# Last stage of a hybrid mixer and expert layer: earlier gathers, residual sums on GpSimd, the last tile stored in halves

## The reference, cut to what matters

```python
out = out + gates[:, e:e + 1] * (he @ p['w_exp_down'][l, e]).astype(f32)   # for each expert e
...
y = _moe(h, l, p)
x = x + gt2 * _rmsnorm(y, p['g_post_ffn'][l])
return x, s_f, s_b
```

## Time and profile before

| | us |
|---|---|
| median of 3 runs | 1619.06 (1616.66 to 1621.87) |
| the profiled execution | 1618.71 |
| its span | 1616.9 |
| TensorE matmul busy | 1392.7 (86%) |
| VectorE busy | 744.0 (46%) |
| ScalarE busy | 238.9 (15%) |
| GpSimd busy | 76.6 (5%) |

### The profile page before, as it was taken

How to read it: one execution, slowest core, us unless ns; L and a number is a source line. 1 busy time by engine, 2 the same in 40 slices (tenths; PEclk the granted TensorE clock), 3 DMA queues, 4 the chain that set the end, 5 groups by cost and what they waited for, 6 DMA issues and landing times.

```text
span 1616.9 us, 13844 instructions
## 1 busy us (share of the span) xinstructions
PE 1392.7 (86%) x5196; PEld 644.3 (40%) x5196; DVE 744.0 (46%) x1245; ACT 238.9 (15%) x390; POOL 76.6 (5%) x127
## 2 busy tenths in 40 slices
PE   2679959999999899999999989589989887899780
PEld 0135524444555445555544434433333333333330
DVE  0135785885776887977873756600000000000005
ACT  0211220100011021111221001411101110111013
POOL 4000000000001000000000000000000000000001
PEclk9799979999999999999999999789989989999995
DMA  9996246675559643122326733999989999999985
GB/s 332 414 358 208 95 146 227 232 244 188 170 176 335 202 142 111 59 85 90 125 97 241 241 135 107 417 348 414 399 335 394 403 403 406 401 406 384 408 357 202
DMA packets 131199, 421.92 MB, mean 261 GB/s; under 512 B 8130, under 2 KB 73893, under 8 KB 113253
## 3 DMA queue, kind: packets, MB, share of 16 engines
q1 hardware_dynamic: 118100, 375.78, 61.4%
q0 software_dynamic: 6656, 32.61, 6.1%
q10 hardware_dynamic: 6384, 12.73, 2.2%
HBM read 409.53 MB, written 23.09 MB: 268 GB/s over the span
## 4 chain that ended last, share of the span: by engine, by line
PE 59%; DMA 21%; DVE 13%; issue 3%; ACT 3%; ACTq 1%; POOLq 0%; SPq 0%; DVEq 0%; POOL 0%
PE ps L497 17%; PE ps L494 14%; DMA s_mem<-in_w_exp_gate 12%; PE ps L823 11%; DMA s_mem<-in_w_ada 7%; PE ps L843 6%; DVE s_mem L1439 4%; DVE s_mem L1604 2%; PE ps L441 1%; PE ps L663 1%; DMA s_mem<-in_hy_freq 1%; DVE s_mem L1576 1%; PE ps L614 1%; PE ps L423 1%; PE ps L625 1%
## 5 line engine op out<-in xcount | busy, mean ns | idle before, releaser
L1439 DVE SCALAR_TENSOR_TENSOR s_mem<-s_mem,s_sT 128x512 f32<-128x512 f32 x480 | 339.4, 748 | 56.8 <-DMA s_mem<-in_w_ada 45.4
L494 PE MATMUL ps<-s_mem 128*128 128x384 f32 x1024 | 343.1, 492 | 1.1 <-DVE s_mem L1470 1.1
L497 PE MATMUL ps<-s_mem 128*128 128x512 f32 x768 | 339.8, 601 | 0.7 <-ACT s_mem L1256 0.7
L823 PE MATMUL ps<-s_mem 128*64 128x512 f32 x1152 | 261.6, 611 | 34.8 <-DMA s_mem<-in_w_exp_gate 34.2
L494 PEld LDWEIGHTS ps<-s_mem 128*128 128x128 f32 x1024 | 193.5, 192 | 142.5 <-issue 18.3
L497 PEld LDWEIGHTS ps<-s_mem 128*128 128x128 f32 x768 | 146.3, 193 | 184.8 <-issue 183.7
L823 PEld LDWEIGHTS ps<-s_mem 128*64 128x64 f32 x1152 | 88.2, 141 | 205.4 <-issue 204.5
L1868 DVE TENSOR_TENSOR s_mem<-s_mem,ps 64x512 f32<-64x512 f32 x18 | 12.2, 680 | 325.4 <-ACT s_mem L1330 325.4
L843 PE MATMUL ps<-s_mem 128*64 128x512 f32 x576 | 152.4, 690 | 9.3 <-DVE s_mem L1870 9.3
L843 PEld LDWEIGHTS ps<-s_mem 128*64 128x64 f32 x576 | 45.5, 157 | 103.0 <-issue 91.1
L1152 ACT ACTIVATE s_mem<-ps 128x512 f32<-128x512 f32 (+1 forms) x61 | 34.4, 581 | 338.3 <-PE ps L497 172.4
(11 more groups left out here) (258 smaller groups left out, 931.9 us busy)
## 6 DMA issues: line engine op xcount, KB each, us to landing
s_mem<-in_w_ada SPq DMA_DIRECT2D x128, 512.0 KB, 5.0
s_mem<-in_w_exp_up SPq DMA_DIRECT2D x32, 2048.0 KB, 33.0
s_mem<-in_w_exp_gate SPq DMA_DIRECT2D x32, 2048.0 KB, 25.8
s_mem<-in_w_exp_down SPq DMA_DIRECT2D x32, 2048.0 KB, 29.5
s_mem<-in_w_in SPq DMA_DIRECT2D x24, 2048.0 KB, 8.8
s_mem<-in_w_ada SPq DMA_DIRECT2D x16, 2048.0 KB, 12.6
s_mem<-in_w_out SPq DMA_DIRECT2D x8, 2048.0 KB, 8.1
y_slots<-s_mem ACTq DMA_DIRECT2D x36, 256.0 KB, 11.2
```

Of the source, the lines that this page charges most:

```text
L494: m = mm(ps[:, banks[m_], 0:TOK], v[:, k, m_ * P:(m_ + 1) * P], hT[:, kk, :], start=(kk == 0), stop=(kk == KT - 1))
L497: m = mm(ps[:, banks[m_], :], hT[:, kk, m_ * P:(m_ + 1) * P], v[:, k, :], start=(kk == 0), stop=(kk == KT - 1))
L823: m = mm(ps[half, 0, :], hgT[:, kh * 8 + k, :], weights(e, 2 * kh + which)[:, k, :], start=(kh + k == 0), stop=(kh * 8 + k == KT - 1), ski ...
L1439: v.op(ve.scalar_tensor_tensor(out=o, in0=w, scalar=scale, in1=o, op0=ALU.mult, op1=ALU.add), S("piece_used") if last else None)
```

## The change

It changes the last stage on four engines.

- GpSimd waits for load 94 in place of load 95, gathers the early rows of tiles 0 and 1, and behind the last block's rows the late rows of both, then tile 2. It takes over the weighing of tile 2 (`last_weighed`) and the residual sums of tiles 0 and 1 (`rows_added`).
- ScalarE weighs tiles 0 and 1 at once; behind the root of each it waits for VectorE's reciprocal (`root_ready`) and scales the tile by it (`z_scaled`).
- VectorE's order becomes combine 0, reciprocal 0, combine 1, reciprocal 1, combine 2, reciprocal 2, and the residual pass of tile 2 in two halves of 1024 columns. Its residual passes of tiles 0 and 1 are gone.
- SyncE stores tiles 0 and 1 behind GpSimd's sums, and tile 2 in two halves.

```diff
 # SyncE
-            for t in range(NT):
-                sp.wait_ge(S("out_ready"), t + 1)
+            for t in range(2):
+                sp.wait_ge(S("rows_added"), t + 1)
                 sp.dma_start(out_rows[t], yga[t][0]).then_inc(S("out_done"), 16)
-            sp.wait_ge(S("out_done"), 16 * NT)
+            for half in range(2):
+                c = slice(half * (D // 2), (half + 1) * (D // 2))
+                sp.wait_ge(S("out_ready"), half + 1)
+                sp.dma_start(out_rows[2][:, c], yga[2][0][:, c]).then_inc(S("out_done"), 16)
+            sp.wait_ge(S("out_done"), 16 * (NT + 1))
 # GpSimd
-            i = LOADS_A_EXPERT * NE - 1
+            i = LOADS_A_EXPERT * NE - 2
             pool.wait_ge(S(f"w{i % len(MOE_SLOTS)}"), 16 * (i // len(MOE_SLOTS) + 1))
-            gather_y(early_i, range(1))
-            for r in range(2):
-                pool.wait_ge(S(f"y_gathered0{r}"), 16)
+            gather_y(early_i, range(2))
+            for t in range(2):
+                for r in range(2):
+                    pool.wait_ge(S(f"y_gathered{t}{r}"), 16)
             pool.wait_ge(S("y_stored"), nblk * 32 + 1)
             pool.nop(nofuse=True)
-            gather_y(late_i, range(1))
-            gather_y(slot_i.rearrange("p r t -> p (r t)"), range(1, NT))
+            gather_y(late_i, range(2))
+            gather_y(slot_i.rearrange("p r t -> p (r t)"), range(2, NT))
+
+            pool.wait_ge(S("y_gathered20"), 16)
+            g.op(nc.gpsimd.tensor_scalar(yga[2][0], yga[2][0], wpair[:, 0, 2:3], None, ALU.mult), S("last_weighed"))
+            for t in range(2):
+                pool.wait_ge(S("z_scaled"), t + 1)
+                g.op(nc.gpsimd.tensor_tensor(yga[t][0], yga[t][1], x_sb[:, t, :], ALU.add), S("rows_added"))
 # ScalarE
             def weigh(t):
-                act.wait_ge(S(f"y_gathered{t}0"), 32 if t == 0 else 16)
+                act.wait_ge(S(f"y_gathered{t}0"), 32)
                 a.op(A(yga[t][0], yga[t][0], ACT.Copy, scale=wpair[:, 0, t:t + 1]), S("y_weighed"))
 
             weigh(0)
+            weigh(1)
             for t in range(NT):
-                if t + 1 < NT:
-                    weigh(t + 1)
                 act.wait_ge(S("y_added"), t + 1)
                 squares(yga[t][0], y_sb[:, 0, :], 32 + t)
                 roots(32 + t, 1, D)
+                if t < 2:
+                    act.wait_ge(S("root_ready"), t + 1)
+                    a.op(A(yga[t][1], yga[t][1], ACT.Copy, scale=stat[:, 32 + t:33 + t]), S("z_scaled"))
 # VectorE
-                dve.wait_ge(S("y_weighed"), t + 1)
+                if t < 2:
+                    dve.wait_ge(S("y_weighed"), t + 1)
+                else:
+                    dve.wait_ge(S("last_weighed"), 1)
                 y0, y1 = yga[t]
-                dve.wait_ge(S(f"y_gathered{t}1"), 32 if t == 0 else 16)
+                dve.wait_ge(S(f"y_gathered{t}1"), 32 if t < 2 else 16)
...
-            def add_residual(t):
+            for t in range(2):
+                combine(t)
                 inverse_roots(32 + t, 1)
-                v.op(ve.scalar_tensor_tensor(out=yga[t][0], in0=yga[t][1], scalar=stat[:, 32 + t:33 + t],
-                                             in1=x_sb[:, t, :], op0=ALU.mult, op1=ALU.add), S("out_ready"))
-
-            combine(0)
-            for t in range(1, NT):
-                combine(t)
-                add_residual(t - 1)
-            add_residual(NT - 1)
+                v.sync()
+                dve.sem_inc(S("root_ready"), 1)
+            combine(2)
+            inverse_roots(34, 1)
+            for half in range(2):
+                c = slice(half * (D // 2), (half + 1) * (D // 2))
+                v.op(ve.scalar_tensor_tensor(out=yga[2][0][:, c], in0=yga[2][1][:, c], scalar=stat[:, 34:35],
+                                             in1=x_sb[:, 2, c], op0=ALU.mult, op1=ALU.add), S("out_ready"))
```

## The result

The change makes the kernel slower, by a third of a per cent: 1623.69 us median of 13 runs against 1619.06 us median of 13 runs of the kernel before on the same chip, ratio 1.0035 (95% interval 1.002 to 1.005), 5.7 us. Forecast was 1620.0 and no measurable change.

A forecast was written before the change was run, and what follows sets the result against it. The 33.7 us tail was taken as set by the gathers' landing, VectorE's passes and 2 MB of final stores. Profiled 1618.71 us plus 1.3 gave 1620.0, range 1614.6 to 1623.0 us.

The forecast's parts named there:

- the exclusion: A VectorE instruction with two SBUF inputs and a GpSimd instruction reading SBUF exclude one another for the whole instruction.
- part 4: GpSimd's passes in the tail: weighing of tile 2 at 2.0 us, residual sums at 4.5 us each, taking turns with VectorE.
- the 1.3 forecast: End of the span: 2 MB of stores from 1611.4 take 6.8 us, ending at 1618.2, 1.3 us over 1616.9.
- Part 1: Waiting for the last load but one, tile 1 gathered early: gathers start about 1564.7, cost 0, unless the load disturbed.
- Rival D: Early gathers and last load disturb one another; 1620.3 us in all; no separate chance, counted with the forecast.
- part 3: ScalarE and VectorE on tiles 0 and 1: new 1.9 us stall before tile 1, whose passes run 1595.55 to 1600.25.
- Part 2: GpSimd's gathers behind 1583.16: tile 1 complete near 1591.0, no longer 1595.8; long 2.76 us issue read as exclusion.
- A: GpSimd's arithmetic and VectorE's two-input passes do not exclude each other in the tail: 1616.2 us, chance 0.28.
- B: GpSimd takes both sums back to back, VectorE's first pass of tile 2 waits until 1609.0: 1621.2 us, chance 0.15.
- C: GpSimd's sums are cheap, near 1.8 us each, so exclusion hardly bites: 1613.0 to 1614.0 us, chance 0.10.

The follow-up runs named there:

- the pairs: Changed kernel plus, behind its last store, GpSimd sums or multiplies each beside three VectorE passes; a sum lengthened three two-SBUF-input passes by 4.1 us (11.11).

## Why the prediction was wrong

It had the order of events, the exclusion and the price of a sum, and missed the size: the time lies 0.7 us above its range.

**The step that failed** is part 4's "For the weighing of tile 2 (one stream in, one out) I take 2.0 us, from 1.8 to 3.6". Measured: 5.44 us. I had priced streams, by the memset; a copy does cost 1.89, but the multiply costs more than the two-input sum. Behind the landing, the weighing was to be done after 16.75 us and was after 20.36 (1601.21): 3.6 us. Everything behind it moved on: tile 2's first pass ended after 27.0 us, not 23.7; sum 1 after 31.4, not 28.2. The range did not carry this term at all: its bounds were worked out from the sum's price, 3.6 to 5.4 us, with the weighing at 2.0 throughout. Even the bound "from 1.8 to 3.6" would have been short by 1.8 us.

**The second term** was not in the sum at all: I had the end 6.85 us behind sum 1, set by the stores. The stores did land 6.55 us behind it, but the end of GpSimd's list set the span, 8.08 us behind it: 1.2 us. 3.2 and 1.2 are the 4.4 us between the forecast tail (35.0) and the measured one (39.45); with the 1.3 forecast, the 5.7. The tails bear both out. With the weighing off GpSimd the tail shrinks by 4.8 us, and with a bare wait at the end of GpSimd's list it grows from 31.0 to 34.9.

**Part 1** held: the gathers alone are worth 2.6 to 2.8 us of tail. But they don't start 0.95 us behind the last load but one (landed 1561.5). The wait that ends last is now the rows of the last block but one:

```profile
1565.25 1.05 POOL L1075 DMA_INDIRECT s_mem<-y_slots,s_early_i  x1 [51.60 <-DMA y_slots<-s_mem]
```

They were there in time all the same, and no matmul waited. Rival D said that part 1 is "worth little more than part 3's stall costs". In the changed kernel it is so: the stall eats it, and tile 1's first pass starts 12.7 us behind the landing, as before (12.75; 10.2 with the gathers alone).

**Part 2 and the exclusion** held; the long gather issue came again (2.78 us), beside the two-input pass, as it was read. **Part 3** held to 0.3 us: stall 2.00, forecast 1.9. **Sum** 4.49, forecast 4.5.

**Rivals.** A (no exclusion) is refuted by the pairs. B did not happen: VectorE's waiting pass ran between the sums each time. Its 1621.2 to 1623.0 us were nearest to the measured time by luck. C is refuted by 4.49 us.

## What to carry to other kernels

Price an operation on GpSimd by that operation in a trace, not by its streams: here a multiply by a scalar costs 5.4 us for 128x2048, more than a sum (4.5) and 2.9 times a copy (1.9). The Trainium skill (GPSIMD Engine Reference, "Engine selection") has one-input operations on GpSimd at roughly line rate; the copy agrees (1.89 us, where ScalarE's weighing takes 2.00), the multiply does not. Moving sums to GpSimd was no relief for VectorE here, whose passes with two SBUF inputs and GpSimd's sums exclude each other; the nine passes on VectorE alone end sooner. Let GpSimd's list end early: in this kernel the execution ends 8 us behind it at the earliest. The best version found is the gathers alone, 2.6 to 2.8 us of tail and 0.11 and 0.12% of time below before, a gain that neither interval tells from none.

## What the runs showed of the hardware that I had not expected

The multiply's price and GpSimd's 8 us, above. And TensorE's clock: ahead of the tail, the same 32 matmuls behind the last gate load took 7.09 us in the kernels before and after, and 10.07 in the first trace with the weighing on ScalarE.

```profile
1560.86 10.07 PE L823 MATMUL ps<-s_mem 128*64 128x512 f32 x32 [3.13 <-DMA s_mem<-in_w_exp_gate]
...
1556.00:1560.00 4.00, 1.72 (x9) 0.29 (x4) 0.00 (x0) 0.00 (x0) 0.00 (x0) 1.00 1.03 437
1560.00:1564.00 4.00, 3.15 (x8) 1.11 (x10) 0.00 (x0) 0.00 (x0) 0.00 (x0) 0.51 1.00 423
1564.00:1568.00 4.00, 4.00 (x14) 1.28 (x12) 0.00 (x0) 0.00 (x0) 0.00 (x0) 0.64 0.98 409
```

The granted clock (third figure from the end, of full speed 2.4 GHz) fell to the lower level, 1.2 GHz, behind a wait of 3.13 us for the load; the kernel before waited 3.13 us at the same place and kept 1.00, and the second trace of the very same kernel waited 3.25 us, kept 1.00 and took 7.09. No kernel changed anything there. So two executions can differ by 3 us ahead of the tail with no cause in the kernel, and an effect of 2 us needs tails, or dozens of runs.
